# Attention outputs of the first two layers turned by their own product, with the linear-attention norm moved behind the attention

## The reference, cut to what matters

```python
y_gla = gla_output(o, g, norm_g)                  # 4 heads of 64: rms_norm per head, gain, * silu(g)
y_na  = neighborhood_attention(nq, nk, nv, nkc, nvc, na_rpb)   # 6 heads of 64
y_swa = sliding_window_attention(sq, sk, sv, skc, svc, swa_sink)  # 6 heads of 64, a sink in the softmax sum
y = jnp.concatenate([y_gla, y_na, y_swa], axis=-1) @ w_out     # 1024 columns, 1024 x 1024 weights
```

## Time and profile before

| what | value |
|---|---|
| time, 3 runs | 3564.52 us median (3563.55 to 3564.6) |
| the profiled execution | 3561.32 us, span 3559.5 us, mean granted clock 0.961 |
| TensorE matmul busy | 3311.6 us, 93% of the span |
| TensorE weight load busy | 2712.8 us, 76% |
| VectorE busy | 2003.3 us, 56% |
| ScalarE busy | 1108.3 us, 31% |
| DMA | 336.23 MB, 94 GB/s over the span |

### The profile page before, as it was taken

How to read it: one execution, slowest core, us unless ns; L and a number is a source line. 1 busy time by engine, 2 the same in 40 slices (tenths; PEclk the granted TensorE clock), 3 DMA queues, 4 the chain that set the end, 5 groups by cost and what they waited for, 6 DMA issues and landing times. The chain is left out here.

```text
span 3559.5 us, 44419 instructions
## 1 busy us (share of the span) xinstructions
PE 3311.6 (93%) x17758; PEld 2712.8 (76%) x17758; DVE 2003.3 (56%) x3615; ACT 1108.3 (31%) x1914; POOL 173.8 (5%) x171
## 2 busy tenths in 40 slices
PE   5997999999999997999999998799999998699998
PEld 4985787888888895787877775567877775478886
DVE  4665655846464434557556556757455557753334
ACT  3113444111112423443222433542222434442222
POOL 0000000000000000000000044000000143000000
PEclk8997999999999997899999999899999999899999
DMA  6341102523231211116444221027444230023332
GB/s 209 126 139 42 52 25 69 154 95 119 89 118 51 72 55 42 52 48 202 155 152 148 81 89 42 1 65 226 151 139 130 75 95 30 0 71 98 95 98 77
DMA packets 316574, 336.23 MB, mean 94 GB/s; under 512 B 11944, under 2 KB 219344, under 8 KB 316368
## 3 DMA queue, kind: packets, MB, share of 16 engines
q1 hardware_dynamic: 316368, 333.39, 30.1%
HBM read 329.67 MB, written 3.67 MB: 94 GB/s over the span
## 5 line engine op out<-in xcount | busy, mean ns | idle before, releaser
L1821 DVE TENSOR_TENSOR weights_low<-weights,weights_high 128x1024 fp32r<-128x1024 f32 (+5 forms) x416 | 488.2, 1176 | 851.7 <-ACT weights_high L1319 849.7
L1319 ACT ACTIVATE weights_high<-weights 128x1024 fp32r<-128x1024 f32 (+5 forms) x416 | 419.8, 1011 | 1314.0 <-PE banks L610 876.2
L1088 PE MATMUL banks<-h_high,weights_high 128*128 128x512 f32 (+1 forms) x1760 | 656.8, 373 | 21.0 <-DVE h_low L1833 12.8
L1088 PE MATMUL banks<-h_low,weights_high 128*128 128x512 f32 (+1 forms) x1760 | 649.7, 369 | 0.0
L1088 PE MATMUL banks<-h_high,weights_low 128*128 128x512 f32 (+1 forms) x1760 | 649.1, 369 | 0.0
L610 PE MATMUL banks<-weights_high,h_high 128*128 128x512 f32 (+4 forms) x1360 | 510.1, 375 | 13.9 <-DVE h_low L1833 9.0
L610 PE MATMUL banks<-weights_high,h_low 128*128 128x512 f32 (+4 forms) x1360 | 501.3, 369 | 0.0
L610 PE MATMUL banks<-weights_low,h_high 128*128 128x512 f32 (+4 forms) x1360 | 499.5, 367 | 0.0
L1088 PEld LDWEIGHTS banks<-h_high,weights_high 128*128 128x128 f32 x1760 | 333.0, 189 | 88.0 <-DVE h_low L1833 14.6
L1088 PEld LDWEIGHTS banks<-h_high,weights_low 128*128 128x128 f32 x1760 | 332.9, 189 | 56.1
L1088 PEld LDWEIGHTS banks<-h_low,weights_high 128*128 128x128 f32 x1760 | 333.3, 189 | 52.9
(11 more groups left out here) (344 smaller groups left out, 4029.7 us busy)
## 6 DMA issues: line engine op xcount, KB each, us to landing
projected<-in_w_mod SPq DMA_DIRECT2D x44, 1024.0 KB, 6.4
weights<-in_w_gate_up SPq DMA_DIRECT2D x88, 512.0 KB, 3.9
weights<-in_w_down SPq DMA_DIRECT2D x80, 512.0 KB, 3.8
extra<-in_w_mod SPq DMA_DIRECT2D x36, 1024.0 KB, 6.4
weights<-in_w_in SPq DMA_DIRECT2D x48, 512.0 KB, 3.7
weights<-in_w_gate SPq DMA_DIRECT2D x44, 512.0 KB, 4.5
weights<-in_w_up SPq DMA_DIRECT2D x44, 512.0 KB, 3.9
weights<-in_w_mod SPq DMA_DIRECT2D x32, 512.0 KB, 3.9
```

The source lines that it names most:

```text
L1088: mm = pe.matmul(bank[:, 0:cnt], wt[:, k, :], x[:, k, a - GOFF:a - GOFF + cnt], start=(k == 0 and q == 0), stop=(k == KD - 1 and q == 2))
L1319: act.activation(WH[s_ % 2][:, 0:k * n], slots[j % LAND][:, 0:k * n], ACT.Copy).then_inc(S["w_high"], 1)
L1821: dve.tensor_tensor(WL[s_ % 2][:, 0:k * n], slots[split_of[s_] % LAND][:, 0:k * n], WH[s_ % 2][:, 0:k * n].bitcast(F32), ALU.subtract).the ...
```

## The change: what it does

In the two layers of the first kind:

- **Values.** v (128 keys x 64) is now loaded and the turned probabilities (128 keys x 128 queries) stream past, so that the output is 64 x 128, turned. The two heads of a pair write the two halves of the output's rows, and their matmuls alternate, key block by key block.
- **Inverse sums.** The sums of a group already stand side by side (`column_of`), so that the six copies go; VectorE inverts them one pair earlier (`inverse`). They must lie along the columns now: behind each group TensorE multiplies each of the six columns, spread over 64, with the identity (six matmuls), ScalarE copies the result to `SPREAD`, and VectorE's `output` multiplies by it.
- **No transposes of blocks 2 to 7.** High and low parts of blocks 2, 3 and 4 are made inside the attention loops (`blocks_beside`, 10, 8 and 6 pairs before its end), those of blocks 5 to 7 behind it; two weight splits are moved into the loops (5 and 4 pairs before the end). The copies reorder the neighborhood's tokens as `by_rows` did.
- **Product order.** Weight units come in the order (2,3), (4,5), (6,7), (0,1). The output product has banks and semaphores of its own (`out_banks`).
- **Norm.** `head_norm` runs on VectorE behind blocks 5 to 7. After the second weight unit TensorE transposes blocks 0 and 1 (`turn_gla`), for which it waits for the norm.
- The scratch layout changes accordingly.

The layers of the second kind keep their values products; they too get the contiguous sums and the earlier `inverse`.

```diff
+        SPREAD = EX[:, 1280:1664]
...
+    def blocks_beside(p):
+        left = len(units) // 2 - p
+        return {10: [2], 8: [3], 6: [4]}.get(left, [])
+    def splits_beside(p):
+        return len(units) // 2 - p in (5, 4)
+    OUT_ORDER = [(2, 4), (4, 6), (6, 8), (0, 2)]
...  TensorE
+                    if nb > 4 and spread[0]:
+                        pe.wait_ge(S["mix_spread_kept"], spread[0])
...
+                def values_of_two(p):
+                    for i in (2 * p, 2 * p + 1):
+                        pe.wait_ge(S["mix_turned_dve" if i % 2 == 0 else "mix_turned_act"], i // 2 + 1)
...
+                    if g and first_of_group(units, 2 * p):
+                        pe.wait_ge(S["mix_out"], g)
+                    for j in range(blocks):
+                        for i in (2 * p, 2 * p + 1):
+                            h, v = units[i]["slot"], units[i]["v"][j]
+                            mm = pe.matmul(PS[7][64 * (h % 2):64 * (h % 2) + 64, 128 * (h // 2):128 * (h // 2) + 128], v,
+                                           PB[i % 4][:, j * PT:(j + 1) * PT], start=(j == 0), stop=(j == blocks - 1))
+                    mm.then_inc(S["mix_values"], 2)
+                    if last_of_group(units, 2 * p + 1):
+                        pe.wait_ge(S["mix_inverse"], g + 1)
+                        if n_fifth(units, 2 * p + 4):
+                            pe.wait_ge(S["mix_fifth"], n_fifth(units, 2 * p + 4))
+                        for f in range(3):
+                            for q in range(2):
+                                mm = pe.matmul(PS[6][64 * q:64 * q + 64, 128 * f:128 * f + 128],
+                                               RCP[:, 2 * f + q:2 * f + q + 1].broadcast_to([PT, 64]), ident, start=True, stop=True)
+                        mm.then_inc(S["mix_spread"], 1)
...
-                pe.wait_ge(S["mixed"], 1)
+                def turn_gla():
+                    pe.wait_ge(S["mix_out"], all_groups)
+                    pe.wait_ge(S["gla_normed"], 1)
+                    (transposes of blocks 0 and 1)
+                for j in range(2):
+                    product(HH, HL, OUT_T, (0, GOFF), 512, 0, KD, lambda i: "d", None if j else there, OB,
+                            lambda u: turn_gla() if (j, u) == (0, 2) else None, low=None, order=OUT_ORDER)
...  ScalarE, in the loop over pairs
+                    if not second:
+                        if p and first_of_group(units, 2 * p):
+                            spread_kept(group_of(units, 2 * p) - 1)
+                        for f in blocks_beside(p):
+                            act.wait_ge(S["mix_out"], na_groups)
+                            turned_high(f)
+                        if splits_beside(p):
+                            split()
...
-                roots(len(OUT_T) * GLA_H)          (before the attention)
+                for f in range(5, KD):             (behind it)
+                    turned_high(f)
+                roots(len(OUT_T) * GLA_H)
...  VectorE
+                    if p and first_of_group(units, 2 * p):
+                        inverse(done)
...
+                        dve.wait_ge(S["mix_values"], i + size)
+                        dve.wait_ge(S["mix_spread_kept"], g + 1)
+                        dve.tensor_tensor(y, PS[7][:, 0:384], SPREAD, ALU.mult).then_inc(S["mix_out"], 1)
...
-                head_norm(...)                     (before the attention)
+                for f in range(5, KD):             (behind it)
+                    turned_low(f)
+                head_norm(...)
+                dve.sem_inc(S["gla_normed"], 1)
+                split()
+                split()
+                (low parts of blocks 0 and 1)
```

More of the change, by code:

```diff
@@ L347, in layer @@
         for k in range(0, KD, 2):
+            k = k if second else (k + 2) % KD
             cols(w["w_out"], 512 * j, 512, k, k + 2)
@@ L547, in layer, with turned_parts @@
     last_filled = []
[L549 to L555, removed]
+    def turned_parts(f):
+        out = []
+        for a, cnt, _ in spans(OUT_T) if f < 5 else [(O0 * PT, len(OUT_T) * PT, 0)]:
+            x = PW[:, a // PT:(a + cnt) // PT, YF[f]:YF[f] + PT]
+            halves = [h[:, f, a - GOFF:a - GOFF + cnt] for h in (HH, HL)]
+            if f < 5 and a:
+                x = x.rearrange("p n (r c) -> p n r c", c=16)
+                halves = [h.rearrange("p (r n c) -> p n r c", r=8, n=4) for h in halves]
+            else:
+                halves = [h.rearrange("p (n q) -> p n q", q=PT) for h in halves]
+            out.append((x, *halves))
+        return out
+    def blocks_beside(p):
[4 more added lines that the diff above has]
+    OUT_ORDER = [(2, 4), (4, 6), (6, 8), (0, 2)]
     with nc.Block() as block:
@@ L1069, in _ @@
                 pe.wait_ge(S["mixed"], 1)
[L1072 to L1082, removed]
+                for f in range(KD):
+                    for a, cnt, r in spans(OUT_T):
+                        bank = B.fill(pe, "d")
+                        for i in range(cnt // PT):
+                            mm = pe.transpose(bank[:, i * PT:(i + 1) * PT], pr(a // PT + i, YF[f], 128), ident)
+                        mm.then_inc(S["filled"], 1)
+                    there[f] = B.emptied_by("d")
+                for j in range(2):
+                    product(HH, HL, OUT_T, (0, GOFF), 512, 0, KD, lambda i: "d", None if j else there)
+                warm(11)
             def gate_up(bank, wh, wl, a, cnt, kk):
@@ L1380, in mixed_out @@
             def mixed_out():
-                for _ in range(3):
+                for _ in range(3 if second else 0):
                     split()
@@ L1700, in _ @@
                 roots(LAT_T * ML_H)
[L1703 to L1711, removed]
+                split()
+                split()
+                for f in range(KD):
+                    for a, cnt, r in spans(OUT_T):
+                        act.activation(HH[:, f, a - GOFF:a - GOFF + cnt], B.share(act)[:, 0:cnt], ACT.Copy).then_inc(S["h_high"], 1)
             mixed_out()
@@ L1948, in softmax_attention @@
                     dve.tensor_copy(PB[2 * p % 4][:, 0:nb], PS[4][:, 0:nb]).then_inc(S["mix_turned_dve"], 1)
+                    if not second and p:
+                        for f in blocks_beside(p - 1):
+                            turned_low(f)
+                        if splits_beside(p - 1):
+                            split()
+                inverse(done)
                 output(done)
@@ L2338, in _ @@
                 softmax_attention()
-                dve.sem_inc(S["mixed"], 1)
+                for f in range(5, KD):
+                    turned_low(f)
+                dve.wait_ge(S["z_loaded"], 16 * len(z_loads))
+                head_norm(PW[:, O0 - T0:, G_Q:G_Q + 256], len(OUT_T), GLA_H, HD, GN, PW[:, O0 - T0:, G_G:G_G + 256])
+                dve.sem_inc(S["gla_normed"], 1)
+                split()
+                split()
+                TG = gla_banks()
+                for f in range(2):
+                    for a, cnt, r in spans(OUT_T):
+                        bank = after_high(TG)
+                        low(f, a, cnt, bank[:, 0:cnt], S["gla_low"])
+                split()
             else:
```

170 lines of the change are left out of this document (112 added, 58 removed).

## The result

| kernel | time, median (lowest to highest) | ratio to before, 95% interval |
|---|---|---|
| before, 4 runs | 3564.03 us (3562.79 to 3564.6) | 1 |
| changed, 4 runs | 3526.11 us (3524.34 to 3528.56) | 0.9903 [0.9884, 0.9921] |
| before beside those of the next row, 11 runs | 3564.55 us (3550.67 to 3572.38) | 1 |
| changed, 6 later runs | 3528.17 us (3525.24 to 3537.31) | 0.9906 [0.9888, 0.9924] |

The account below looks back on a forecast made before the run. TensorE's issue was taken as the bound. Attentions -18.1, attention to product -8.5, ahead of attention -1.1 sum to -27.7 us: 3533.6 us profiled, 3536.8 us median; own range 3526 to 3548, whole range 3517 to 3560.

Parts of the forecast that it names:

- Values: Attention values matmuls: two heads overlap side by side, 0.0533 us a record instead of 0.1155, gaining 56.7 us.
- Drains: Attention pairs: changes of tiling drain TensorE and take 22.5 of the 56.7 us, leaving 34.2.
- The 0.29: Between transposes and values of each pair: changing into column tiles costs 0.29 us, read from a 128 x 32 block.
- drain rule: TensorE in the attention: changing the tiling mode, not just the tile, drains it; by this rule 34 us gained.
- Groups: Behind each of 20 attention groups: six more matmuls plus waits at five-block and two-block groups, 16.1 us added.
- the 0.4 us of missing slack: Groups with two key blocks: no slack for the added group work, so 0.4 us lost, four times.
- the forecast's -18.1: Both attentions together: -34.2 us from the values after drains, +16.1 us from the groups' new work.
- Inserted blocks and splits at nothing: Inside the attention loops: making blocks 2 to 4 and two weight splits costs nothing, at most 3 us.
- From the attention to the product: Last values to output product: product starts at once, gaining 5.9 us in layer 0 and 2.6 in layer 1.
- Layer 0 does not wait: `turn_gla` in layer 0: norm done 15.6 us behind the last values, two weight units end at 17.1, so no wait.
- Ahead of the attention: Before first scores: moving the norm gains 1.1 us in layer 0, nothing in layer 1, where gathers set the start.
- rival 4: Clock at 1.2 GHz for a seventh of the attentions: some 23 us come back, 3560 us, no change; chance 0.06.

Follow-up runs that it names:

- e1: Changed kernel with a pair's values matmuls issued head by head instead of alternating by key block: 3552.37 us, ratio 0.998 to the kernel before.
- e4: Changed kernel with the values placed between the transposes of a pair's two units, one more tiling change per pair: 3546.05 us, ratio 0.9948 to before.
- e5: Changed kernel with each group's spreading matmuls issued twice into the same banks: 3541.46 us, ratio 0.9929 to the kernel before.
- e6: Changed kernel with the work on blocks 2 to 4 and two weight splits moved behind the attention: 3546.65 us, ratio 0.9943 to the kernel before.
- third profile: Changed kernel, unedited, timed in the same rounds as two variants and profiled again: 3528.17 us, ratio 0.9906 to the kernel before.
- e3: Changed kernel with the low parts of blocks 0 and 1 made ahead of the second weight split: 3526.46 us, ratio 0.9905 to the kernel before.
- e9: Changed kernel with ten warm-up matmuls for six before the linear-attention products, and blocks 0 and 1's low parts before the second weight split: 3517.03 us, ratio 0.9869.
- first profile: Changed kernel as first measured and profiled: median 3526.11 us, span of the profiled execution 3522.6 us.
- second and third: Two later profiles of the unedited changed kernel: 3531.45 us and 3528.17 us.
- second profile: Kernel before, unedited, profiled once more: 3562.68 us.
- e2: Changed kernel with the linear-attention norm and its roots back ahead of the attention: 3527.47 us, ratio 0.9908 to the kernel before.

## Why the prediction was right, and where not

**Values.** Right as taken: 0.053 us a record (0.0533 used). e1 shows that this hangs on the order of issue. The pace before was set a little high, 0.1155 us where 1.83 us for 16 records give 0.114: this makes the forecast gain 1.0 us too large.

**Drains.** The mechanism was right, the size too large. The values' start waits 0.17 us and not 0.29, their end 0.17 and not 0.14: 3.11 us for 3.20, 3.76 for 3.85. The 0.29 was the distance from the start of a 426-column matmul at full width to the first narrow tile; that part of it was this matmul itself is likely but was not tested. Over 36 pairs of four and 12 of five blocks this is some 4.2 us more gain. The drain rule weighed in the prediction (Trainium skill, TensorEngine Tiling (Array Packing), Key Properties) holds: e4 adds one change and the period grows by 0.15 us.

**Groups.** 16.1 us forecast (its terms add up to 16.0). The first periods are longer by 0.65 (12 of four blocks), 1.24 (4 of five) and about 0.5 (4 of two): 14.8. e5 shows the matmuls uncovered; the wait for the fifth copies is there with 0.38 us as said; for two blocks the 0.4 us of missing slack did not come. The table gives -23.9 us for the attentions, but it ends them at the last values, while the forecast's -18.1 has the last spread of each layer in it, 1.3 us together. Counted alike it is -22.6 for -18.1. Drains (4.2) and groups (1.3), less the 1.0 of the values, are these 4.5.

**Inserted blocks and splits at nothing.** Right (e6).

**From the attention to the product.** Forecast -5.9 and -2.6 us. The table has -2.6 (-1.1 in the third profile) and -2.3; without the last spread, which the forecast books with the groups, -3.3 and -2.9. Layer 1 came as said. In layer 0 the step that failed reads "Layer 0 does not wait". The norm was counted rightly (done 15.2 us behind the last values, 15.6 forecast), but not the moment at which a third bank would be free, behind a split that had been called "needed one unit later". The two waits of the turning, 2.15 and 0.16 us, are 2.3 of the missing 2.6. e3 and e9 show the price, 1.2 to 2.9 us, and that the order alone removes it; two waits of some 0.5 us are left.

**Ahead of the attention.** -1.1 and 0 forecast; -2.6 and within the scatter (-1.1 to +0.5) found. The gathers were the next bound, as said (0.34 us of wait for them in layer 0, first profile), but the warm-up behind them took 1.98 us and not 3.1, at the full clock. In layer 1 it took 1.98 us behind a wait of 1.75 (first profile), and 3.22 and 3.45 behind waits of 2.73 and 2.96 (second and third), where the granted clock falls to 0.50 during it.

**The sum.** Like for like, with the linear attention at its long lengths in both kernels, the span goes from 3560.2 (mean of two) to 3529.7 us: -30.5, beside -27.7 forecast. The terms -22.6, -6.2 and -2.6 make -31.4. The measured medians show 36 to 38; the first profile's further 6.5 us are the clock's in an untouched stage. No term of the forecast has them, so that the measured time lay as low as the range's edge is in part luck. Among nine profiles of the changed kernel and its variants with that stage's code, layer 1 had the short length in seven; before had it in neither of two. Whether the kernel before meets it more rarely is open, and with it 5 to 7 us of the median; 7 of its 35 later runs lie 6 us or more below its second profile, so it has shorter executions too, but none of them has a trace. So rival 4 was right that the clock would move microseconds, but at a pause outside the change and in the other direction. (Its own 23 us do not follow from its condition: a seventh of some 209 us of attention done at half the clock would add 30.)

## What to carry to other kernels

Two heads with 64-column outputs side by side halve the values' time only if their matmuls alternate in the order of issue; here this was needed for eight and ten records a head and made no difference for four. Book 0.17 us for each change of tiling, and place small matmuls next to others of the same tiling. When work moves behind another stage, follow every bank and every split in the order of the engine that frees it, not only the result that is waited for. Before a gain is believed, compare stretches that the change cannot touch: here one of them carried a sixth of it in the first profile, and filling the pause that made it vary lowered the median by another 4 to 6 us, in ranges that still overlap.

## What the runs showed of the hardware

- Two 128-row, 64-column tiles: 0.053 us a record alternating. Head by head the records of one head stand 0.109 us apart and the two heads overlap by four records: 0.084 us on average with eight records a head, no loss with four.
- A change of tiling left the load unit idle for 0.17 us from full width to 64 columns, from 64 columns back to full width (e4), and from 64 columns to 64 rows; one change more lengthened the period by 0.15 us.
- A pause of 4.35 us of TensorE had two outcomes for the same kernel, 2.4 GHz again within 4 us or 1.2 GHz for some 10 us more: 3.2 us of difference in that stage, and over 10 in the profile of e3. A wait of 2.15 us (2.43 in e2) left the clock up in three profiles and was followed by 1.2 GHz in six; waits of 0.57 and 0.48 us left it up in two.
